# Sample rows merged into 64 stationary columns, forget rows and v loads moved, the down stage of TensorE written out

## The reference, cut to what matters

```
z = x @ w_in                      # one projection, 4176 columns
h_m = mlstm(mq, mk, mv, mo, gates)   # 4 heads of 128, matrix memory, carried over the tokens
h_a = sparse_attention(aq, ak, av, indexer iq, ik, iw)   # 8 heads of 64, top 256 keys of each query
x1 = layer_norm(ALPHA * x + concat(h_m, h_a) @ w_out)
y  = layer_norm(ALPHA * x1 + (silu(x1 @ w_gate) * (x1 @ w_up)) @ w_down)
```

## Time and profile before

| | |
|---|---|
| median of 3 runs | 1614.91 us (1614.64 to 1616.3) |
| profiled execution | 1615.25 us, span 1613.5 us |
| granted clock of TensorE | 0.994 of 2.4 GHz on average |
| PE busy | 1564.4 us, 97% of the span |
| DVE, ACT, POOL busy | 762.3, 448.5 and 406.8 us |

### The profile page before, as it was taken

The page is one execution under the profiler, slowest core; times in us unless marked ns, Lnnn a source line. Parts: engine busy times, 40 slices in busy tenths (PEclk is TensorE's granted clock), DMA queues, the critical chain, the costliest instruction groups (busy, mean ns, idle before and its releaser), DMA issues.

```text
span 1613.5 us, 27249 instructions
## 1 busy us (share of the span) xinstructions
PE 1564.4 (97%) x10677; PEld 1446.8 (90%) x10677; DVE 762.3 (47%) x1655; ACT 448.5 (28%) x929; POOL 406.8 (25%) x394
## 2 busy tenths in 40 slices
PE   7999999999998998889999999999999999999998
PEld 7996799999996666587789999999999999999986
DVE  2008599999934665553553314223132322413146
ACT  4336433222144565362352111211212021111100
POOL 3530155321210002434493212212221221122200
PEclk9999999999999999899999999999999999999999
DMA  5210231223216103624203111111111110111012
GB/s 184 69 45 15 67 100 35 73 62 106 80 64 244 34 22 110 175 87 160 79 1 90 42 53 53 34 46 53 54 30 50 53 54 27 53 53 53 1 53 82
DMA packets 117085, 110.65 MB, mean 69 GB/s; under 512 B 16187, under 2 KB 102207, under 8 KB 116963
## 3 DMA queue, kind: packets, MB, share of 16 engines
q1 hardware_dynamic: 116322, 106.80, 21.4%
q0 software_dynamic: 640, 2.10, 0.4%
HBM read 88.82 MB, written 19.95 MB: 67 GB/s over the span
## 4 chain that ended last, share of the span: by engine, by line
PE 55%; issue 0%; DVE 0%; ACT 0%; DVEq 0%
PE bank L1766 32%; PE bank L1744 13%; PE bank L1544 6%; PE bank L1931 3%; PE bank L1926 0%; PE bank L1684 0%; PE bank L1140 0%; PE bank L1126 0%; PE bank L1143 0%; DVE hidden L1849 0%; ACT silu L1811 0%; PE bank L1155 0%; DVE y_tm L1967 0%; DVE y_tm L1959 0%; DVE stats L1950 0%
## 5 line engine op out<-in xcount | busy, mean ns | idle before, releaser
L1766 PE MATMUL bank<-x_split,gate_up_split 128*128 128x352 f32 x3168 | 510.8, 323 | 3.4 <-DVE hidden L1849 2.4
L1766 PEld LDWEIGHTS bank<-x_split,gate_up_split 128*128 128x128 f32 x3168 | 507.4, 188 | 4.3 <-DVE hidden L1849 3.0
L2210 PE MATMUL bank<-w_split,xT_split 128*128 128x256 f32 (+1 forms) x2160 | 274.3, 285 | 2.2 <-ACT w_split L2282 1.8
L2210 PEld LDWEIGHTS bank<-w_split,xT_split 128*128 128x128 f32 (+1 forms) x2160 | 259.4, 181 | 8.5 <-issue 3.1
L1849 DVE TENSOR_TENSOR hidden<-silu,bank 128x352 f32<-128x352 f32 x66 | 34.4, 521 | 412.5 <-ACT silu L1811 412.4
L1744 PE MATMUL bank<-hidden_split,weight_split 128*128 128x352 f32 x1296 | 209.1, 322 | 0.0
L1744 PEld LDWEIGHTS bank<-hidden_split,weight_split 128*128 128x128 f32 x1296 | 207.9, 188 | 0.0
L1885 POOL TENSOR_TENSOR gate_up_split<-gate_up,gate_up_split 128x2048 fp32r<-128x2048 f32 x22 | 104.3, 4739 | 377.7 <-ACT gate_up_split L1803 377.7
L2515 DVE TENSOR_SCALAR_CACHE_REDUCE chosen<-scores,level 128x384 uint8<-128x384 f32 (+2 forms) x198 | 174.3, 942 | 1.2
L1752 DVE TENSOR_TENSOR y_acc<-y_acc,bank 128x352 f32<-128x352 f32 x216 | 112.5, 521 | 84.6 <-PE bank L1744 83.4
L2267 PE MATMUL bank<-xT_split,w_split 128*128 128x352 f32 x864 | 138.7, 323 | 1.2 <-ACT feature_stage L2383 1.2
(11 more groups left out here) (294 smaller groups left out, 1636.8 us busy)
## 6 DMA issues: line engine op xcount, KB each, us to landing
w_unit<-in_w_in_dram SPq DMA_DIRECT2D x16, 1024.0 KB, 5.7
gate_up<-in_w_gate_dram SPq DMA_DIRECT2D x22, 512.0 KB, 4.0
gate_up<-in_w_up_dram SPq DMA_DIRECT2D x22, 512.0 KB, 5.3
down_weight<-in_w_down_dram SPq DMA_DIRECT2D x11, 1024.0 KB, 5.1
scratch_dram<-feature_stage SPq DMA_DIRECT2D x36, 176.0 KB, 1.8
scores<-in_x_prompt_dram SPq DMA_DIRECT2D x8, 512.0 KB, 5.4
out_dram<-stage SPq DMA_DIRECT2D x32, 128.0 KB, 1.7
out_weight<-in_w_out_dram SPq DMA_DIRECT2D x16, 256.0 KB, 6.9
```

What stands on the lines that cost most here:

```text
L1766: mm = pe.matmul(PS[2 * c + w][:, 0:CH], gs[u][:, a, w, k, :], xs[:, b, k, c * CH:(c + 1) * CH], start=(k == 0 and (a, b) == PARTS[0]), st ...
L2210: mm = pe.matmul(bank[0:rows(i), 0:HALF], xs1[:, a, k, tile_cols(i)], w[:, b, k, :], start=((k, a, b) == terms[0]), stop=((k, a, b) == ter ...
```

## The change

1. **Sample tile in 64 columns.** For seven of the eight depth steps (k = 0 to 6) the high and the low part of the 32 sample tokens lie side by side as 64 stationary columns. Two matmuls (with the high and with the low weights) replace three, and write the product of the high part to the rows 0 to 31 of the bank and that of the low part to 32 to 63. k = 7 keeps its three matmuls of 32 columns, and is done before k = 6. So a tile `LAST` has 17 matmuls and not 24, in ten `tm` units and in both halves of `pe_product`. The low x low product is added by this.
2. **What this needs.** When x is turned, ACT and DVE write the sample's parts a second time side by side (three operations each); the same holds for mix. ACT empties both halves of the bank (one operation more), POOL adds them (`sum_halves`, 32x256, `sample_summed`); in the output product DVE does so with a second addition. ACT's emptying of a tile `LAST`, of `scd` and of the first `fm` job now also waits for these sums, the stores of av and mv of the tile `LAST` too.
3. **Forget rows.** `act_forget` is moved from job 18 to job 27 of the `fm` jobs, `act_decay` from 27 to 33.
4. **v loads.** SP's wait for the `fm` stores is moved behind the nine v loads, ahead of the loads for the mLSTM.
5. **mLSTM outputs.** For the chunks 5 to 8 DVE scales the outputs, by one operation of 128x512 behind the denominator, and ACT doesn't.
6. **FFN on PE.** The loop of four turns is written out: eight bodies in a row. The loops of the other engines stay.

```diff
+        def sample_parts(j, bank, part):
+            src = bank.rearrange("p (k n) -> p k n", k=4)[:, :, 0:SMP]
+            half = slice(SMP * part, SMP * part + SMP)
+            if j == 0:
+                return [(xs_0to3[:, :, :, half], src.rearrange("p (c k) n -> p c k n", c=2))]
+            return [(xs_45[:, :, half], src[:, 0:2, :]), (xs_6[:, :, half], src[:, 2:3, :])]
...
+            for s in range(FST):
+                sp.wait_ge(fstored[s], 16 * (len(fm_no) // FST))
             sp_mlstm_loads(sp)
...
-                take_outputs(n)
+                if n <= MH:
+                    take_outputs(n)
...
                 dve.reciprocal(inv, both).then_inc(den_done, 1)
+                if n > MH:
+                    dve.wait_ge(den_done, n + 1)
+                    dve.wait_ge(h_ps, n - 1)
+                    o = o_banks[:, :, 0:2 * VE].rearrange("p b (i n) -> p b i n", n=VE)[:, :, :, 0:P]
+                    dve.tensor_tensor(htm[:, n % 2].rearrange("p (b i) n -> p b i n", b=2), o,
+                                      inv.unsqueeze(3).to_broadcast([P, 2, 2, P]), ALU.mult).then_inc(o_taken, 2)
...
+            order_k = list(range(KD)) if i < LAST else [0, 1, 2, 3, 4, 5, 7, 6]
+            for k in order_k:
...
+                if i == LAST and k < KD - 1:
+                    for b in range(2):
+                        mm = pe.matmul(product_bank(m)[0:2 * SMP, :], split_mix(k), wo[h][:, k, b, :],
+                                       start=(k == 0 and b == 0), stop=(k == 6 and b == 1))
...
+                if i == LAST:
+                    total.then_inc(sample_summed, 1)
+                    dve.wait_ge(sample_summed, len(sample_no) + h + 1)
+                    total = dve.tensor_tensor(x, product_bank(m)[r:2 * r, :], x, ALU.add)
+                total.then_inc(added, 1)
...
-            with pe.Fori(0, (GROUPS - 3) // 2) as j:
-                body(j * 2 + 1, 1)
-                body(j * 2 + 2, 0)
-            body(GROUPS - 2, 1)
+            for g in range(1, GROUPS - 1):
+                body(g, g % 2)
...
-            for s in range(FST):
-                sp.wait_ge(fstored[s], 16 * (len(fm_no) // FST))
             sp_rest(sp)
...
+                        terms = [(k, a, b) for k in ks for a, b in PARTS if i < LAST or a == 0 or k == KD - 1]
...
+                            if i == LAST and k < KD - 1:
+                                out, tokens = bank[0:2 * SMP, 0:HALF], split_sample(k)
...
-                if job == ("fm", "mq", 2, 0):
+                if job == ("fm", "mo", 1, 0):
                     act_forget(act)
-                if job == ("fm", "mo", 1, 0):
+                if job == ("fm", "mo", 3, 0):
                     act_decay(act)
...
+                        if sample_no[job]:
+                            act.wait_ge(sample_summed, sample_no[job])
+                        act.activation(st[0:SMP, :], bank[0:SMP, 0:HALF], ACT.Copy)
+                        out = act.activation(low_of(job), bank[SMP:2 * SMP, 0:HALF], ACT.Copy)
...
                 elif kind == "scd":
+                    act.wait_ge(sample_summed, 4)
...
+                    if f == 0:
+                        act.wait_ge(sample_summed, len(sample_no))
...
+            def sum_halves(job):
+                pool.wait_ge(freed, pos[job] + 1)
+                both = stage[0:SMP, stage_no[job] % STG, :]
+                pool.tensor_tensor(both, both, low_of(job), ALU.add).then_inc(sample_summed, 1)
...
                     low(4)
+                    sum_halves(("tm", "av", 1, LAST))
```

More of the change, by code:

```diff
@@ L270, in build, with low_of @@
         idx_no = {j: r for r, j in enumerate(idx_jobs)}
+        sample_no = {j: n for n, j in enumerate(j for j in staged if j[3] == LAST and j[1] != "ik")}
+        def low_of(j):
+            return low_half[j[1] in ("ak", "aq", "mv")]
         turned_into = dict(iq=iqT, ik=kiT, ak=kT, aq=qT)
@@ L1542, in pe_product @@
                     pe.wait_ge((mix_lo_pool, mix_lo_dve)[i % 2], 2 * (i // 2) + k // 4 + 1)
[L1543 to L1545 removed]
+                if i == LAST and k < KD - 1:
+                    for b in range(2):
+                        mm = pe.matmul(product_bank(m)[0:2 * SMP, :], split_mix(k), wo[h][:, k, b, :],
+                                       start=(k == 0 and b == 0), stop=(k == 6 and b == 1))
+                else:
+                    for a, b in PARTS:
+                        mm = pe.matmul(product_bank(m)[0:rows(i), :], mix(i, a)[:, k, :], wo[h][:, k, b, :],
+                                       start=(k == 0 and (a, b) == PARTS[0]), stop=(i < LAST and k == KD - 1 and (a, b) == PARTS[-1]))
                 if between and k == 3:
@@ L1563, in mix_high @@
             for j in range(2):
-                act.activation(mix(i, 0)[:, 4 * j:4 * j + 4, :], mixT[:, 4 * j:4 * j + 4, tile_cols(i)], ACT.Copy)\
-                    .then_inc(mix_hi, 1)
+                whole = [(mix(i, 0)[:, 4 * j:4 * j + 4, :], mixT[:, 4 * j:4 * j + 4, tile_cols(i)])]
+                for dst, src in whole if i < LAST else sample_mix(j, 0):
+                    a = act.activation(dst, src, ACT.Copy)
+                a.then_inc(mix_hi, 1)
         def mix_low(eng, i, done):
@@ L1571, in mix_low @@
                 eng.wait_ge(mix_hi, 2 * i + j + 1)
-                eng.tensor_tensor(mix(i, 1)[:, k, :], mixT[:, k, tile_cols(i)], mix(i, 0)[:, k, :].bitcast(F32), ALU.subtract)\
-                    .then_inc(done, 1)
+                whole = [[(mix(i, part)[:, k, :], mixT[:, k, tile_cols(i)])] for part in range(2)]
+                for (hi, src), (lo, _) in zip(*(whole if i < LAST else [sample_mix(j, 0), sample_mix(j, 1)])):
+                    low = eng.tensor_tensor(lo, src, hi.bitcast(F32), ALU.subtract)
+                low.then_inc(done, 1)
         def out_high(act, h, j):
@@ L2320, in _ @@
                                          bank[:, :].rearrange("p (k n) -> p k n", k=4)[:, :, 0:rows(i)], ACT.Copy)
+                    for dst, src in sample_parts(j, bank, 0) if i == LAST else ():
+                        out = act.activation(dst, src, ACT.Copy)
                 elif kind == "tm":
@@ L2403, in rope_tile @@
                 sin = rope[0:r, i, 1, :].unsqueeze(1).to_broadcast([r, hn, 16])
-                pool.wait_ge(freed, pos[job] + 1)
+                if i == LAST and g != "ik":
+                    sum_halves(job)
+                    pool.wait_ge(sample_summed, sample_no[job] + 1)
+                else:
+                    pool.wait_ge(freed, pos[job] + 1)
                 if steps:
```

52 lines of the change are left out of this document (42 added, 10 removed).

## The result

The changed kernel takes 1590.35 us (median of 4 runs, 1588.97 to 1590.79), the kernel before 1615.61 (1614.64 to 1617.43): a ratio of 0.9845, with an interval of 0.9832 to 0.9859, or 25.3 us less. The forecast was 1590.5 us, between 1587 and 1600. The profiled execution of the changed kernel is its fastest, 1588.97 us with a span of 1587.3; against the span of before that is 26.2 less.

A forecast was written before the change was run, and what follows sets the result against it. TensorE, busy for 97% of the span, was taken to bound the kernel. Six terms, 6.2 + 1.2 + 4.8 + 4.8 + 3.2 + 4.35 = 24.6 us, from 1615.25 gave 1590.7, or 1590.5 against the median; range 1587 to 1600.

The forecast's parts named there:

- (a): Projection's tiles LAST: seven fewer matmuls give 0.85 us per tile, none at iq 0 and av 1; 6.2 us in all.
- (b): Forget rows at the feature jobs: moved later, DVE's row has long been there, so PE's wait goes; 1.2 us.
- (c): v loads before the attention's first values: issued 3.4 us earlier, PE's wait and the slower clock after it go; 4.8 us.
- (d): mLSTM outputs: DVE scaling instead of ACT removes PE's waits of 2.63 and 0.46 and the lower clock behind; 4.8 us.
- (e): Output product: seven fewer matmuls in each of two halves, 0.231 us per matmul; 3.2 us.
- (f): FFN loop on PE: written-out bodies remove the gaps at the loop's three returns; 4.35 us.
- Absorbed: Rival: ACT's and POOL's chains keep their pace and PE meets them earlier; 9.2 us less gain, about 1599.7; chance 0.17.
- Switching columns costs: Rival: in tiles LAST, 26 column-width changes cost 0.16 us each, 4.2 in all, about 1594.7; chance 0.09.
- DVE's scaling does nothing: Rival, mLSTM: DVE's own queue holds the state back, so scaling there gains 0; about 1595.3; chance 0.06.
- The written-out bodies stream worse: Rival, FFN: 6,912 instructions in a row bring pauses; the whole gain gone, or 1639 at twice that; chance 0.05.

The follow-up runs named there:

- better: Changed kernel with three pieces of weight splitting moved (one on ACT, two on POOL): 1588.55 us, ratio 0.9832 to the kernel before.

## Why the prediction was right, point by point

The time, the range and the direction held, and each term can be found in the table of stages. (Against the median the sum gives 1590.4 and not 1590.5; nothing hangs on this.)

- **(a) and (b)**, 6.2 + 1.2 = 7.4: the stretch up to the attention is 9.04 shorter. About 1.5 of it is no part of the change: TensorE reached the first sample tile at 44.13 and not at 45.64, with nothing altered ahead of it but what hangs on the first loads. 7.5 are left. The run without merging has (b) too; counted from its own first sample tile, at 43.54, it takes 6.1 us more than the changed kernel, which is (a), and 1.4 less than before, which is (b). That the gain dies at iq 0 and av 1 came out as told.
- **(c)**, 4.8: 4.63 between the two profiled executions, but not by part 4 alone: that gives 2.5 at this place in the trace of the kernel before, and 1.4 in the changed one. Most of the 4.63 comes with the merging as well: alone, with the wait still in its place, it has 12.94 us here and not 16.44, since the last store lands sooner. The price was read from a wait that the change shortened twice; that the sum met it is in part luck.
- **(d)**, 4.8: 5.06 in the table, 5.6 by undoing it. The table's stage varies by itself: in seven other runs whose last chunks are scaled by DVE it took 63.3 to 65.7 us, and the changed kernel's 62.44 is the shortest, so 5.06 is in part the luck of one execution. The mechanism holds in every trace: the brackets of 0.46 and 2.6, with the lower clock behind them, stand in all five kernels whose last chunks ACT scales and in none of the eight where DVE does.
- **(e)**, 3.2: 3.28, and **(f)**, 4.35: 4.26.

The rivals. *Absorbed* is refuted by the run without the merging (9.4 for it). *Switching columns costs* is refuted by 0.03 for four changes. *DVE's scaling does nothing* is refuted by the 5.6 of undoing it. *The written-out bodies stream worse* is wrong in its sign: they run without one idle piece, and it is the loop whose returns depend on where the code stands.

One step of the working failed, without a price: under (b), that at the new place of `act_forget` the row "has long been there". It ended 1.1 us after ACT had come there (452.27 and 451.16), and only ACT's table load hid this, since DVE's search took 260.5 us and not 250.1, with more of its operations standing behind POOL's splits. I had taken DVE's pace as given. What the sum hid is larger: it holds because all parts came together. The runs that leave one out lose 17.9, 2.1, 16.4, 5.6 and 9.4, 51.4 together, for a change worth 25.3; what the mLSTM varies by itself, up to 3 us in each, can't explain this. Part 3, with a term of 1.2, is what lets the merging through; part 6, with 4.35, guards against a loop that the merging would have made worse. A forecast for the merging alone, made by the same sums, would have said 9.4 faster, and it is 15.7 slower.

What stays open: why DVE's steps fall on POOL's splits as they do in each kernel, and whether the instruction load is what slows the last store.

## What to carry to other kernels

When an engine that sets the pace gets faster, look for the place where it meets one that doesn't: a bracket of 1.2 us there grows by all that is gained ahead of it, and moving the waiting instruction is worth the whole of that gain. Terms of a sum are prices in the kernel before, with nothing else changed; a part with a small term may be what the others rest on, so a change of several parts is to be tried with each part left out, not only put in. Before a loop's return is priced from a trace, know that the price belongs to the place of its code, and that removing instructions far ahead of it can more than triple it (4.26 and 15.2 us here).

## What the runs showed of the hardware

- The return of TensorE's loop costs 1.0 to 1.6 us between two matmuls in one place of the code (3.7 to 4.3 for three returns), and in another 1.0 to 1.6 and then 2.3 to 2.7 three matmuls later, with some ten matmuls at 1.2 GHz behind (15.2 to 15.7 for three). A shift of 24 instructions turns the second into the first.
- An operation of DVE on 128x6 elements that takes 0.17 us stands for up to 4.5 when it starts while POOL subtracts 128x2048 elements (4.6 us): all 83 that took over 0.4 us in the 13 traces ended 0.02 to 0.04 us behind an operation of POOL. DVE's search takes 249 to 261 us by how its steps fall on these; the same code took 250.1 and 248.7 in two kernels.
- Matmuls of 32, 64 and 128 stationary columns take the same time for the same streamed columns (24 of 512 columns 5.54 us with 32 and 5.59 with 128; 17, most of them with 64, 3.92: 0.23 each), and four changes between 32 and 64 cost 0.03 us.
- The mLSTM, 62 to 66 us with DVE scaling its last chunks, differs by where TensorE is granted 1.2 GHz. In the run with more changes of width the stretch from 679.6 to 682.8 us was at 0.50, with 17 matmuls; in the changed kernel the same stretch was at 1.00, with 32. The widths are not the reason: the last run above (`better`), which has those of the changed kernel, has such a stretch at the same place (676.6 to 679.8, at 0.50, 16 matmuls).
